# Attention of block 2: score steps shifted by one unit, and the 256- and 128-key probabilities transposed side by side and copied once

## The reference, cut to what matters

```
s  = einsum('bghqd,bgkd->bghqk', q, k) * scale     # scores of 128 queries with their causal keys
p  = softmax(where(mask, s, NEG_INF))              # "sel", "win": rotated q, k; "fox": with forget-gate sums
o  = einsum('bghqk,bgkd->bghqd', p, v)
o  = gate_cmp * o_cmp + gate_sel * o_sel + gate_win * o_win    # nsa heads
o  = p_fox @ v_fox                                             # fox heads
mix = concatenate([o_nsa, o_fox]) @ w_out
```

## Time and profile before

| | |
|---|---|
| median of 3 runs | 1665.84 us (1665.37 to 1665.9) |
| the profiled execution's own time | 1665.28 us |
| its span in the trace | 1663.5 us |
| PE busy, share of the span | 1604.9 us, 96% |
| DVE, ACT, POOL busy | 67%, 43%, 34% |
| attention of layer 1, first scores to last values | 490.5 to 608.3 us of the span |
| attention of layer 2, first scores on | from 1144.3 us of the span |

### The profile page before, as it was taken

One profiled execution on the slowest core, in us unless ns is written; L12 is line 12 of the kernel. 1 busy time (PEld: TensorE's weight loads), 2 busy tenths in 40 slices (PEclk: granted clock), 3 DMA queues, 4 the chain that ended last, 5 costly groups with the idle time before them and its releaser, 6 DMA issues.

```text
span 1663.5 us, 25186 instructions
## 1 busy us (share of the span) xinstructions
PE 1604.9 (96%) x9415; PEld 1255.4 (75%) x9415; DVE 1111.5 (67%) x1963; ACT 709.5 (43%) x1428; POOL 570.7 (34%) x592
## 2 busy tenths in 40 slices
PE   7988999999999999999999999999999999999997
PEld 3455547477776778988888878777677889999886
DVE  7999766345346655887788655554674588888944
ACT  4334342244236644544443334334673444444431
POOL 1010000232205654444444725111663444444460
PEclk9999999999999999999999999999999999999999
DMA  6324230054411003333333314432000433333321
GB/s 194 77 26 96 49 136 1 1 140 145 109 51 52 2 13 102 113 97 97 101 102 102 94 49 141 143 82 102 2 1 13 129 107 97 100 102 102 102 89 51
DMA packets 195979, 137.69 MB, mean 83 GB/s; under 512 B 35063, under 2 KB 177138, under 8 KB 195858
## 3 DMA queue, kind: packets, MB, share of 16 engines
q1 hardware_dynamic: 189564, 128.86, 26.5%
q10 hardware_dynamic: 6294, 7.22, 1.9%
HBM read 131.00 MB, written 2.10 MB: 80 GB/s over the span
## 4 chain that ended last, share of the span: by engine, by line
PE 77%; DVE 15%; ACT 3%; issue 2%; POOL 1%; DMA 1%; SPq 0%; ACTq 0%; POOLq 0%; DVEq 0%
PE ps L570 15%; PE ps L571 15%; PE ps L572 14%; PE ps L2131 5%; PE ps L2132 5%; PE ps L2133 5%; PE ps L2001 4%; PE ps L1206 3%; PE ps L2017 3%; PE ps L2034 2%; ACT BIG L2303 2%; PE ps L1886 1%; PE ps L1114 1%; DVE WH_MLP L555 1%; PE ps L612 1%
## 5 line engine op out<-in xcount | busy, mean ns | idle before, releaser
L572 PE MATMUL ps<-HT_R,WR_R 128*128 128x512 f32 (+1 forms) x832 | 313.1, 376 | 0.0
L572 PEld LDWEIGHTS ps<-HT_R,WR_R 128*128 128x128 f32 x832 | 156.8, 188 | 31.7
L570 PE MATMUL ps<-HT_R,UP_HI 128*128 128x512 f32 x448 | 177.3, 396 | 0.0
L571 PE MATMUL ps<-HL_MLP,UP_HI 128*128 128x512 f32 x448 | 177.0, 395 | 0.0
L492 DVE TENSOR_TENSOR WR_R<-WR,UP_HI 128x1024 fp32r<-128x1024 f32 x56 | 98.8, 1765 | 100.2 <-ACT UP_HI L486 100.2
L2201 ACT ACTIVATE BIG<-ps 64x512 f32<-64x512 f32 (+4 forms) x110 | 62.8, 574 | 169.9 <-PE ps L572 152.1
L2756 POOL TENSOR_TENSOR U_LO<-BIG,U_HI 128x768 fp32r<-128x768 f32 (+1 forms) x48 | 116.5, 2449 | 23.6 <-DVE BIG L2607 21.8
L900 PE MATMUL ps<-WR,HT 128*128 128x512 f32 (+1 forms) x256 | 112.6, 590 | 1.2 <-ACT BIG L1683 1.2
L530 ACT ACTIVATE WH_MLP<-BIG 128x1024 fp32r<-128x1024 f32 x48 | 51.0, 1062 | 143.1 <-DVE BIG L540 143.1
L2131 PE MATMUL ps<-WH_MLP,U_HI 128*128 128x256 f32 x384 | 108.5, 283 | 2.2 <-DVE WH_MLP L555 2.2
L2727 POOL TENSOR_SCALAR BIG<-BIG,rg,gate 128x512 f32<-128x512 f32 (+2 forms) x96 | 62.8, 667 | 138.5 <-DVE rg L2559 138.5
(11 more groups left out here) (414 smaller groups left out, 4262.3 us busy)
## 6 DMA issues: line engine op xcount, KB each, us to landing
WR<-in_w_up SPq DMA_DIRECT2D x64, 512.0 KB, 4.0
WR<-in_w_down SPq DMA_DIRECT2D x96, 256.0 KB, 3.3
WR<-in_w_in SPq DMA_DIRECT2D x36, 512.0 KB, 5.3
WR<-in_w_out SPq DMA_DIRECT2D x6, 2048.0 KB, 8.0
WR<-in_w_in SPq DMA_DIRECT2D x5, 2048.0 KB, 10.1
WR<-in_w_down SPq DMA_DIRECT2D x16, 512.0 KB, 3.7
WR<-in_cmp_w_k SPq DMA_DIRECT2D x8, 512.0 KB, 5.3
WR<-in_cmp_w_v SPq DMA_DIRECT2D x8, 512.0 KB, 4.9
```

What stands on the lines that cost most here:

```text
L570: nc.tensor.matmul(out_, w[0], x[0], start=start, stop=False)
L571: nc.tensor.matmul(out_, w[0], x[1], start=False, stop=False)
L572: return nc.tensor.matmul(out_, w[1], x[0], start=False, stop=stop)
```

## The change

The outer loop on PE starts at -1, so that a step has the scores of B and C, and the next those of D and of the next group's A. `turn_of` numbers the transposes' turns, three for a group: A, B, and C with D. D's blocks go behind C's in banks 4 and 5 (`turn_col`), and one copy of 2 x 384 columns takes both. The turns, not the units, now alternate between DVE (even turns) and ACT (odd): in groups with even k DVE copies A and CD, and ACT copies B; in groups with odd k it is the other way round. There are 36 copies in a layer where there were 48. In the step that holds the scores of B and C, the values now stand ahead of both turns of transposes.

```diff
+        NTURN = 3 * (NU2 // 4)
+        turn_of = lambda u: 3 * (u // 4) + (0, 1, 2, 2)[u % 4]
+        turn_units = lambda g: [4 * (g // 3) + i for i in ((0,), (1,), (2, 3))[g % 3]]
+        turn_col = lambda u: P * (t_of(u - 1) + 1) if u % 4 == 3 else 0
+        turn_width = lambda g: sum(P * (t_of(u) + 1) for u in turn_units(g))
...
-            def turned_copied(u):
+            def turned_copied(g):
-                pe.wait_ge((sem.pT_dve, sem.pT_act)[u % 2], NU2 // 2 * l + u // 2 + 1)
+                pe.wait_ge((sem.pT_dve, sem.pT_act)[g % 2], NTURN // 2 * l + g // 2 + 1)
...
-                if u:
-                    turned_copied(u - 1)
+                if u and turn_units(turn_of(u))[0] == u:
+                    turned_copied(turn_of(u) - 1)
...
-            for u in range(0, NU2 + 6, 2):
+            for u in range(-1, NU2 + 6, 2):
                 for s in (u, u + 1):
-                    if s < NU2:
+                    if 0 <= s < NU2:
                         scores(s)
-                if u == 0:
+                if u == -1:
                     wide_product(proj_bank(23), 23, HL_IN, k_to=4)
+                if u % 4 == 1:
+                    for before in (u - 5, u - 4):
+                        if 0 <= before < NU2:
+                            values(before)
                 for z in (u - 3, u - 2):
                     if 0 <= z < NU2:
                         probabilities_turn(z)
...
-                    if z == u - 3:
+                    if z == u - 3 and u % 4 != 1:
                         for before in (u - 5, u - 4):
                             if 0 <= before < NU2:
                                 values(before)
...
-                    if o == 0 and 0 <= z < NU2 and z % 2:
+                    g = turn_of(z)
+                    if o == 0 and 0 <= z < NU2 and g % 2 and z == turn_units(g)[-1]:
                         act.wait_ge(sem.pT_ps, NU * l + 2 * z + 2)
...
-                if 0 <= u - 3 < NU2 and (u - 3) % 2 == 0:
-                    turned_even(u - 3)
+                z = u - 3
+                if 0 <= z < NU2 and z == turn_units(turn_of(z))[-1] and turn_of(z) % 2 == 0:
+                    turned_even(turn_of(z))
```

More of the change, by code:

```diff
@@ L2016, in probabilities_turn @@
                     for b in range(t_of(u) + 1):
-                        last = nc.tensor.transpose(ps[4 + o][:, P * b:P * b + P], PR[u % 4][:, o, P * b:P * b + P], ident[:])
+                        c = turn_col(u) + P * b
+                        last = nc.tensor.transpose(ps[4 + o][:, c:c + P], PR[u % 4][:, o, P * b:P * b + P], ident[:])
                     last.then_inc(sem.pT_ps, 1)
@@ L2030, in values @@
                     pe.wait_ge(sem.o_sb, NH * l + group - 1)
-                turned_copied(u)
+                turned_copied(turn_of(u))
                 for b in range(t + 1):
+                    c = turn_col(u) + P * b
                     for o in range(2):
                         last = nc.tensor.matmul(o_bank(group)[HD * o:HD * o + HD, P * t:P * t + P], v_of(kind, 2 * j + o, b),
-                                                PT[u % 3][:, o, P * b:P * b + P], start=(first and b == 0),
+                                                PT[turn_of(u) % 3][:, o, c:c + P], start=(first and b == 0),
                                                 stop=(b == t), skip_group_check=True)
@@ L2304, in two_act @@
                                              scale=-1.0, accum_out=rs[:, 2 * u + o:2 * u + o + 1]).then_inc(sem.s_exp, 1)
-                    if o == 0 and 0 <= z < NU2 and z % 2:
+                    g = turn_of(z)
+                    if o == 0 and 0 <= z < NU2 and g % 2 and z == turn_units(g)[-1]:
                         act.wait_ge(sem.pT_ps, NU * l + 2 * z + 2)
-                        if z >= 3:
-                            act.wait_ge(sem.o_ps, NU2 * l + z - 2)
-                        n = P * (t_of(z) + 1)
-                        copy(PT[z % 3][:, :, 0:n], psum[:, 4:6, 0:n]).then_inc(sem.pT_act, 1)
+                        if g >= 3:
+                            act.wait_ge(sem.o_ps, NU2 * l + turn_units(g - 3)[-1] + 1)
+                        n = turn_width(g)
+                        copy(PT[g % 3][:, :, 0:n], psum[:, 4:6, 0:n]).then_inc(sem.pT_act, 1)
                 if u == NU2 + 3:
@@ L2544, in masked_least, with turned_even @@
                                                3.0e38, ALU.add, ALU.min, mn[:, i:i + 1]).then_inc(sem.s_masked, 1)
-            def turned_even(z):
-                dve.wait_ge(sem.pT_ps, NU * l + 2 * z + 2)
-                if z >= 3:
-                    dve.wait_ge(sem.o_ps, NU2 * l + z - 2)
-                w = P * (t_of(z) + 1)
-                nc.vector.tensor_copy(PT[z % 3][:, :, 0:w], psum[:, 4:6, 0:w]).then_inc(sem.pT_dve, 1)
+            def turned_even(g):
+                dve.wait_ge(sem.pT_ps, NU * l + 2 * turn_units(g)[-1] + 2)
+                if g >= 3:
+                    dve.wait_ge(sem.o_ps, NU2 * l + turn_units(g - 3)[-1] + 1)
+                w = turn_width(g)
+                nc.vector.tensor_copy(PT[g % 3][:, :, 0:w], psum[:, 4:6, 0:w]).then_inc(sem.pT_dve, 1)
             def one_over_sum(u):
```

## The result

The changed kernel takes 1703.87 us (median of 4, 1700.83 to 1705.24) where the kernel before took 1665.87 (1665.37 to 1667.91) beside it: a ratio of 1.0223, with a 95% interval of 1.021 to 1.0236. It is slower, as predicted, but by 38 us and not by 19; the time lies outside the range of 1673 to 1693. The profiled execution took 1705.24 us, 39.96 more than the one before.

The account below looks back on a forecast made before the run. Bound: a loop through PE, DVE and ACT, 8.47 us a group. Per layer +5.6 (groups 1-6), +0.65 (7), +1.1 (8), +1.8 (9-10), +0.4 (ends): +9.6, twice +19.2; forecast 1685 us, range 1673 to 1693.

Parts of the forecast that it names:

- an even group costs more, an odd one not: In sel and win groups: even k takes 10.45 us for 8.47, +1.98; odd k takes 8.37, -0.10.
- The marks set down: Profile signs: periods alternating about 10.4 and 8.4 us, PE waits 0.7 and 0.5, score waits, DVE and ACT 2 lower.
- C's second wait until 7.46 and take 0.43 (half of 0.85): Even group: C's second scores wait for the next A's second exponential until 7.46 us, then take 0.43, ending at 7.89.
- without a partner beside them, take half of 1.70: Even group: A's second scores, running alone from 1.36 us, take 0.85 and end at 2.21.
- at about 0: Even group: C's first exponential on ACT ends at about the end of C and D's transposes, time 0.
- scores of B and C 1.27: Odd group: PE's scores of B and C, 640 keys, take 1.27 us, from 4.54 to 5.81.
- just when B's scores end: Odd group: the next A's second exponential is through at about 5.3 us, as B's scores end.
- in group 10 a split of the output weights ... now it sits on the loop: Fox group 10: DVE's 1.30 us weight split stands between A's copy and the next A's mask; groups 9 and 10 +1.8.
- -1 to +2, I take +0.4: A layer's first and last groups: half a projection ahead of B and C's scores, one wait for B's copy; +0.4 us.
- only one of the two stalls counts: Rival, chance 0.24: A's heads still overlap, so an even group loses 0.75 us less; -7.5 in all, 1677.
- even groups go like odd ones: Rival, chance 0.06: DVE's copy of A doesn't delay the next mask; sel and win groups 8.4 us, total 1665 to 1669.
- covers hold: Rival, chance 0.10: PE's own work sets the period, sel and win groups at best 7.69 us; up to -9, 1656.

Follow-up runs that it names:

- turns-first version: The changed kernel with the transposes of C and D ahead of the values of A and B in the B-and-C scores step; 1695.72 us.
- the copy of CD moved late: The changed kernel with ACT's copy of CD behind C's second exponential instead of between C's two exponentials; 1696.55 us.
- rearranged version: The changed kernel with PE's steps reordered to give every copy a cover, ACT copying A and DVE copying B and CD; 1673.23 us.

## Why the prediction was right and where it was wrong

**Bound and direction: right.** The period through PE, DVE and ACT was the thing to read, and "an even group costs more, an odd one not" decided the sign. The marks set down were met: periods that alternate, PE waiting for the copy ahead of B's transposes (0.51 us of PE's time behind DVE's copy at 548.58, 0.31 behind ACT's; 0.7 and 0.5 were forecast), the two waits of scores. The busy times weren't: PE's was to stay and rose by 25 us; DVE's and ACT's were to fall by 2 each, and DVE's fell by 1.7 (1111.5 to 1109.8) while ACT's rose by 3.7 (709.5 to 713.2), since ACT now copies half of the A's.

**The chain itself: right, with one kind of step too cheap.** From A's transposes to C's second scores an even group takes 551.48 - 546.17 = 5.31, by the prediction 7.46 - 2.21 = 5.25. Transposes of A to those of B: 2.41 and 2.21 against 2.47 and 2.25. ACT's copy of 1024 columns takes 1.02, by the line 1.01. What was off is "C's second wait until 7.46 and take 0.43 (half of 0.85)" and "without a partner beside them, take half of 1.70". A head that has lost its partner costs as much as both side by side. Both heads of A(0) take 494.01 - 492.95 = 1.06 us; one head of A alone takes 1.06 too (545.11 to 546.17, and 535.55 to 536.61 in the odd group). C's second took 0.63 (551.48 to 552.11), which is what the line through 1.70 for 896 and 0.85 for 384 keys gives for both heads of 256. The halves were 0.85 and 0.43, so 0.21 and 0.20 were missing. Besides, C's first exponential was to end "at about 0" and ended 0.19 later (543.80 - 543.61), so that A's second scores started at 1.50 where 1.36 stood, and at 0.80 for 0.62 in the odd group. And "scores of B and C 1.27" took 1.51 in the odd group (539.62 to 541.13), since C's second head starts behind A's second exponential, which the prediction had called "just when B's scores end". Less the values and other small differences, these make +0.53 in an even and +0.49 in an odd group. In the turns-first version, where the heads of A meet again, A's part of them is gone. They are 5.4 of the 19.6 us by which the two profiled attentions (38.8 us longer) exceed the 19.2 forecast.

**Fox: group 10 right in place, short by the clock.** "in group 10 a split of the output weights ... now it sits on the loop" named the right cost; groups 7 to 10 cost +5.5 a layer and not +3.55, nearly all of it in group 10 (13.83 for 12.1). 1.6 of that 1.7 is the clock, by the two windows above. 3.9 us in all, 3.2 of them the clock.

**First and last groups: the step that failed.** "-1 to +2, I take +0.4" was +6.4 and +4.8, 10.4 us of the 19.6. 2.9 us a layer pass before A(0)'s transposes start (8.90 for 6.04): B(0)'s scores stand behind half a projection, which the prediction said and put no sum to, and the transposes stand behind A(1)'s scores. 1.2 a layer are the evacuation: A(1)'s scores now come ahead of the projection's second half, so that its exponential is ready early and stands behind an evacuation that can't start. I had looked at ACT's copies there and not at what else it has to do. 2.6 and 1.1 are the clock. Together 6.7 and 5.2; the rest of the layer gave 0.3 back. So the orders alone, 2.9 + 1.2, were already twice the upper bound of 2.

**The clock: put at nothing.** It stood in no term of the sum. Before, it was full over both attentions; in the change, stretches at 0.77 to 0.91 appear at the start and in group 10. They cost about 7.0 us of the 19.6 (contained in the two paragraphs above). What makes it fall isn't shown: it fell behind waits of PE, but the same instructions with the same waits ran at the full clock in another trace.

**Rivals.** That only one of the two stalls counts is refuted by the copy of CD moved late (0.70 of the 2.12; the rest is left for the copy of A). That even groups go like odd ones isn't so, but a kernel in which they do is 25 us faster. That covers hold came nearest to true in the rearranged version, 8.06 for 8.47 with 7.69 as the floor. The range left out the result because the high end gave the start 2 us, and the unpaired heads and the clock nothing.

## What to carry to other kernels

When a loop's order is shifted, list for every engine whatever else is tied to a unit's number there, the evacuations and splits too, and follow each across the shift; the middle of the loop is the easy part. Ask of a copy what covers it and whose mask or exponential stands behind it on its engine: who makes the copy of A was worth 45 us here, while twelve copies fewer in a layer could not be told from none (+57.5 and +59.8, with A on DVE). And two matmuls that run side by side don't split into two halves when one of them must wait: the one left alone costs as much as the pair.

## What the runs showed of the hardware that I had not expected

- Two heads of 64 rows side by side, 512 keys, took 1.06 us (492.95 to 494.01), and one head of A alone 1.06 as well; one of C alone took 0.63. D and A together took 1.28 us when all were released, 1.86 to 2.52 when the second head of A waited.
- The granted clock can fall behind short waits and need not. After 2.29 us in which PE was idle came 3.5 us at 0.51, with matmuls 0.43 us apart instead of 0.23; at the start of the change it fell behind waits of 0.98 and 0.08 us, and with the same waits it stayed full in the version with the copy of CD late. At the lower level eight transposes took 1.82 us instead of 1.09, 28 value records 3.14 instead of 1.68.
- An edit that shortens two groups by 2.2 us (the splits moved) was worth nothing, since the next wait and the clock behind it took as much.
